# A decoder layer on one core: sum T2 in halves, another order of high parts, and two low parts on GpSimd, in the first up unit

## The chip, the cores and the metric

The kernel runs on one core of one Trainium2 chip. The time is what the device takes for one execution, in microseconds (us); lower is better. The core's engines run their own instruction streams side by side and meet at semaphores: TensorE (PE, with its weight loads PEld), VectorE (DVE), ScalarE (ACT), GpSimd (POOL) and SyncE (SP), which here only issues transfers.

## The reference, cut to what matters

One layer of a hybrid decoder on x of 1024 tokens by 1024 features, all float32. The change lies in the first half of the MLP (the up projection):

```
h = rms_norm(x) * (1.0 + scale2) + shift2
x = x + gate2 * (jnp.square(jax.nn.relu(h @ w_mlp_in[l])) @ w_mlp_out[l])   # w_mlp_in 1024 x 4096
return rms_norm(x) * final_norm_g
```

Ahead of it stand the conditioned norm, the combined projection, windowed attention, gated linear attention and the output projection, which the change does not touch.

## The kernel before, in words

**Precision.** A float32 operand is split in two: a high part (the value rounded to fp32r, one ScalarE copy) and a low part (value minus high part, one VectorE tensor_tensor). A product is three matmuls: high by high, high by low, low by high.

**Tiles.** The up projection h @ w_mlp_in is computed by a seven-product scheme of the Strassen-Winograd kind. h (turned, features on the partitions) is four quarters called 11, 12, 21 and 22, each 128 x 4 x 512: the first digit is the half of the features, the second the half of the tokens. Four sums are made of them: T1 = 12 - 11, T2 = 22 - T1, T3 = 22 - 12, T4 = 21 - T2. The sums lie in place of operands: T1 over 11, T3 over 12, T4 over T2 (`h_full`). The seven operands 11, 21, T1, T2, T3, T4, 22 each get a high and a low part, in two halves of 128x1024 (`form_hi`, L2182 on ScalarE, counted by s_hhi; `form_lo`, L1639 on VectorE, counted by s_hlo). The sums are `form_sum`, L1643, 128x2048, counted by s_hsum.

**Units.** There are NU = 8 units of weight columns. Each has seven weight forms (numbered f = 7u + i), of 128x1024 each: `wide_hi(f)`, L2146 on ScalarE, counted by s_whi, and `wide_lo(f)`, L1599 on VectorE, counted by s_wlo. Four buffers go round for them. TensorE runs the seven products in the order 11, 21, T1, T2, T3, T4, 22 (`up_product`, L1148), each in two halves m of 12 matmuls of 128x512, into two PSUM banks. Product i of unit u starts when s_wlo has reached f + 1 and, in unit 0 only, when the operand's low half has been counted by s_hlo: the first half before its k = 0, the second before its k = 2. The operands of h are made once, in unit 0, so this unit is the one in which TensorE waits for them.

**Banks.** Three products, T2's, T3's and T4's, add on top of one another in the same two banks as product 11 (X_UP). Between them ScalarE must copy what a bank holds: `kept`, L2214, 128x512 a bank. T2's product waits for the copy of 11's (s_p1), T3's for the copy of T2's (s_u2), T4's for the copy of T3's (s_u3).

**Order.** No scheduler decides anything: each engine's stream is in the order of its code. In unit 0, VectorE's goes: sum T1, low form 2, low T1, an affine (a scaled and shifted copy out of PSUM, 128x512, L1630), low form 3, sum T2, low T2, sum T3, low form 4, low T3, sum T4, low form 5, low T4. ScalarE's goes: high T1, three affines (L2166), the copies of 11's banks, high T2, high forms 4 and 5, high 22, high T3, the copies of T2's banks, high form 6, high T4. The tuple `H_HI_ORDER` repeats ScalarE's order, so that VectorE's `form_lo` waits for the right count of s_hhi. SP starts the loads of unit 1's weights when sums T2 and T4 are made, since they overwrite 11 and 21 (L531, L533). GpSimd has no work from the end of the linear attention to the down projection: it waits at s_prod, 14 * NU.

Of the kernel before, what the change touches and what calls it, by code (L numbers as in the profile page):

```python
# [87 lines left out]
UP_STARTS = (True, True, True, False, False, False, False)  # L88
UP_H = ("11", "21", "T1", "T2", "T3", "T4", "22")
H_ORDER = ("11", "21", "T1", "T2", "T3", "T4", "22")  # L90
H_HI_ORDER = ("11", "21", "T1", "T2", "22", "T3", "T4")
AFF_S = ((0, 0), (0, 2), (0, 4), (0, 5), (0, 6), (0, 7), (1, 0), (1, 2), (1, 4), (1, 5), (1, 6))
AFF_V = ((0, 1), (0, 3), (1, 1), (1, 3), (1, 7))
UP_P1, UP_P2, UP_P5, UP_P6, UP_P7, UP_P4, UP_P3 = range(NP)
# [62 lines left out]
def build(nc, x, c, w_ada, b_ada, w_in, w_gate_up, b_gate, gla_norm_g, attn_sinks, rel_bias,  # L157
# [236 lines left out]
    with block:  # L394

        @block.sync
        def _(sp):
# [130 lines left out]
                sp.wait_ge(s_free, G_O + 8 + t + 1)  # L528
                sp.dma_start(x1_rows[:, t, :], x1[:, t, :]).then_inc(s_x1_out[t // 4], 16)
            sp.wait_ge(s_hlo, 2 * (H_ORDER.index("T1") + 1))  # L530
            sp.wait_ge(s_hsum, 2)  # L531
            up_load(1, (0,))
            sp.wait_ge(s_hsum, 4)  # L533
            up_load(1, (1,))

            def hid_sums_store(u):
# [57 lines left out]
        @block.gpsimd  # L594
        def _(pool):
            pool.memset(ones[:, :], 1.0).then_inc(s_set, 1)
            pool.wait_ge(s_set, 1)
            pool.memset(rel_ext[BUCKETS:BUCKETS + 1, :], LOWEST).then_inc(s_set, 1)
            pool.wait_ge(s_set, 2)
            pool.memset(gate1[:, 512:D], 0.0).then_inc(s_set, 1)  # L600
            pool.wait_ge(s_ada_first[2 * NCK - 1], 32)
            pool.wait_ge(s_ada_full, 2)
            for part in range(2, 6):
                if part in gate_rows:
                    if part == 5:
                        pool.wait_ge(s_ada_sum, 1)
                    pool.dma_start(ada_b[0:1, :], b_ada[0:1, part * D:(part + 1) * D]).then_inc(s_ada_b, 16)
                for k in range(KT):
                    j = (part - 2) * KT + k
                    if j >= 4:  # L610
                        pool.wait_ge(s_ada_used, j - 3)
                    pool.dma_start(ada_w[:, j % 4, :], w_ada_d[:, k, part * D:(part + 1) * D])\
                        .then_inc(s_ada_w[j % 4], 16)
            pool.wait_ge(s_ada_used, 4 * KT)
            pool.memset(w_gate[:, :], 0.0).then_inc(s_set, 1)
            pool.wait_ge(s_set, 5)
            for r in range(COPIES):
                pool.dma_start(w_gate[r * COL:r * COL + RANK, :], w_gate_up[0]).then_inc(s_wg, 16)
            with nc.allow_non_contiguous_dma(reason="128 gains, one a partition"):
                pool.dma_start(gain_col, gla_norm_g[0].rearrange("(p a) -> p a", a=1)).then_inc(s_gn, 16)  # L620

            pool.wait_ge(s_gate_v, 10)
            pool.memset(a_mask[:, :, :], 0.0).then_inc(s_zeros, 1)
            pool.memset(state_a[:, :, :], 0.0).then_inc(s_zeros, 1)
            pool.memset(prob[:, :, 0:P], LOWEST).then_inc(s_zeros, 1)

            for n in range(NT):
                pool.wait_ge(s_g_copy, n + 1)
                pool.tensor_scalar(g_low[:, :], g_copy[:, :], -1.0, 0.0, ALU.mult, ALU.max).then_inc(s_pool, 1)
                pool.wait_ge(s_pool, n + 1)  # L630
                pool.wait_ge(s_sg_e, n + 1)
                pool.tensor_tensor(silu_g[:, :], silu_g[:, :], g_low[:, :], ALU.add).then_inc(s_sg_sum, 1)
                pool.wait_ge(s_sigmoid, n + 1)
                pool.tensor_tensor(silu_g[:, :], g_copy[:, :], silu_g[:, :], ALU.mult).then_inc(s_sg, 1)

            def dn_load(dst, block_of, q, landed):
                j, l = block_of
                for k in range(2):
                    pool.dma_start(dst[:, 2 * k:2 * k + 2, :],  # L639
                                   w_down_d[j, q][:, 2 * k:2 * k + 2, l * HALF:(l + 1) * HALF]).then_inc(landed, 16)  # L640

            def dn_ring_load(r):

                q = r % NQ
                if r >= 2:
                    step = (NQ * DN_P2, NQ * DN_P4, NQ * DN_P3)[(r - 2) // NQ] + (r - 2) % NQ
                    pool.wait_ge(s_dlo, 4 * step + 4)
                dn_load(dn_ring[r % 2], ((1, 0), (1, 0), (1, 1))[r // NQ], q, s_dn_ring[r % 2])

            def dn_ab_load(q):  # L650
                dn_load(dn_a[:, q], (0, 1), q, s_dn_ab[q])
                dn_load(dn_b[:, q], (1, 1), q, s_dn_ab[q])

            def residual_again(*tiles):
                for t in tiles:
                    pool.dma_start(x1[:, t, :], x1_rows[:, t, :]).then_inc(s_x1_back[t // 4], 16)

            pool.wait_ge(s_prod, 14 * NU)
            dn_ring_load(0)
            dn_ring_load(1)  # L660
            for form in range(NP):
                pool.wait_ge(s_hid_out[form], 16 * NU)
            for q in range(NQ):
                pool.wait_ge(s_dlo, 4 * q + 8)
                dn_ab_load(q)
            for r in range(2, 6):
                dn_ring_load(r)
            pool.wait_ge(s_dlo, 4 * (NQ * DN_P5 + 4))
            residual_again(0, 1, 2, 3)
            pool.wait_ge(s_dlo, 4 * (NQ * DN_P7 + 2))  # L670
            residual_again(4, 5, 6, 7)
            pool.dma_start(gain[:, :], final_norm_g.rearrange("(a d) -> a d", a=1).broadcast_to([P, D]))\
                .then_inc(s_gfin, 16)
            for r in range(6, 3 * NQ):
                dn_ring_load(r)
# [538 lines left out]
        def _(v):  # L1214
# [381 lines left out]
            def wide_lo(f):  # L1596

                v.wait_ge(s_whi, f + 1)
                v.tensor_tensor(up_lo[f % 4][:, :, :], up_form(f), up_hi[f % 4][:, :, :], ALU.subtract).then_inc(s_wlo, 1)  # L1599
# [85 lines left out]
            form_lo("T1")  # L1685
            v.wait_ge(s_x1_out[1], 64)
            affine(1, 7)
            wide_lo(3)
            v.wait_ge(*h_ready(1, 6))
            v.wait_ge(*h_ready(1, 7))  # L1690
            v.wait_ge(s_hsum, 1)
            form_sum("T2", "22", "T1")
            form_lo("T2")
            form_sum("T3", "22", "12")

# [42 lines left out]
            for u in range(NU):  # L1738
                f = NP * u
                if u > 0:  # L1740
                    up_add(u - 1, HID_S3, Z_UP, s_u2, UP_P3, s_c12)
                    wide_lo(f + 3)
                    hidden_sums(u - 1)
                    wide_lo(f + 4)
                    up_add(u, HID_11, Y_UP, s_p1, UP_P2, s_c11)
                    wide_lo(f + 5)
                    wide_lo(f + 6)
                else:
                    wide_lo(4)
                    form_lo("T3")  # L1750
                    v.wait_ge(s_hsum, 2)
                    form_sum("T4", "21", "T2")
                    wide_lo(5)
                    form_lo("T4")
                    up_add(u, HID_22, Z_UP, s_u3, UP_P5, s_c22)
                    wide_lo(6)
                    form_lo("22")
                    wide_lo(7)
                    up_add(u, HID_11, Y_UP, s_p1, UP_P2, s_c11)
                    v.wait_ge(s_hlo, 2 * NP)  # L1760
                next_sum(u + 1, 0)
                next_sum(u + 1, 1)
                if u > 0:
                    next_lo(f + 7)
                next_sum(u + 1, 2)
                if u == NU - 1:
                    down_lo(0)
                if u > 0:
                    up_add(u, HID_22, Z_UP, s_u3, UP_P5, s_c22)
                next_lo(f + 8)  # L1770
                next_sum(u + 1, 3)
                next_lo(f + 9)
# [146 lines left out]
        def _(a):  # L1919
# [250 lines left out]
            def form_hi(name):  # L2170

                for j in range(2):
                    ks = slice(2 * j, 2 * j + 2)
                    if name in ("11", "21", "22"):
                        half, k = int(name[1]) - 1, 4 * (int(name[0]) - 1) + 2 * j
                        a.wait_ge(*h_ready(half, k))
                        a.wait_ge(*h_ready(half, k + 1))
                    else:
                        a.wait_ge(s_hsum, int(name[1]))
                    if name == "T4":  # L2180
                        a.wait_ge(s_hlo, 2 * (H_ORDER.index("T3") + 1))
                    a.activation(h_hi[name][:, ks, :], h_full[name][:, ks, :], ACT.Copy).then_inc(s_hhi, 1)  # L2182
# [90 lines left out]
            for u in range(NU):  # L2273
                f = NP * u
# [8 lines left out]
                if u == 0:  # L2283
                    form_hi("T2")
                    wide_hi(4)
                    wide_hi(5)
                    form_hi("22")
                    form_hi("T3")
                    for m in range(2):
                        kept(HID_S3, u, m, UP_P6, s_u2)  # L2290
                    wide_hi(6)
# [99 lines left out]
```

## Time and profile before

| what | value |
|---|---|
| median of 3 runs | 1056.14 us (1054.41 to 1058.13) |
| the profiled execution's own time | 1054.87 us |
| its span, first to last instruction | 1053.1 us |
| TensorE busy | 1027.5 us, 98% |
| VectorE busy | 707.8 us, 67% |
| ScalarE busy | 474.5 us, 45% |
| GpSimd busy | 95.4 us, 9% |
| mean granted TensorE clock | 0.998 |

The trace's clock starts at the first instruction; the profiled execution is 1.8 us longer than its span. In rows of a timeline the first number is the start, the second the length from the first start to the last end of a run of like instructions, and x is their count; consecutive instructions on one engine overlap by about 0.1 us as shown, so a step is the difference of two starts. What stands in brackets is the engine's idle time before, and what ended it. TensorE's ends are modelled. Spans on GpSimd are rough. The granted clock is 1.00 of full speed through the up units.

### The profile page before, as it was taken

The numbers are of one execution on the slowest core, as the hardware profiler recorded it, in microseconds if no ns is written. First come the engines' busy times: TensorE is split into PE (matmuls) and PEld (weight loads), VectorE is DVE, ScalarE is ACT, GpSimd is POOL, SyncE is SP. The second block draws the span as 40 slices with busy tenths as digits, with TensorE's granted clock in tenths as the row PEclk, the third lists the DMA queues.
The fourth block names the chain that finished last, engine by engine and source line by source line (L and its number), as shares of the span: only waits on it lengthen the run. The fifth ranks groups of instructions, "written<-read, shape, count | busy, mean of one in ns | idle before, by whom it ended". The sixth has DMA issues, their size and how long they took to land.

```text
span 1053.1 us, 12994 instructions
## 1 busy us (share of the span) xinstructions
PE 1027.5 (98%) x5027; PEld 822.7 (78%) x5027; DVE 707.8 (67%) x926; ACT 474.5 (45%) x786; POOL 95.4 (9%) x123
## 2 busy tenths in 40 slices
PE   6999999999998999999999999999999999999997
PEld 4677887766676788878888888888888888888885
DVE  4576668788987264897555555554549963578886
ACT  7321012377776102765544544445453434335343
POOL 0111210022323000000000000000231000001100
PEclk9999999999999999999999999999999999999999
DMA  9977731300001613128345335327997332554633
GB/s 333 313 218 267 259 123 41 81 1 1 1 1 68 213 41 140 60 82 301 138 140 179 140 121 180 139 82 280 355 375 253 113 120 80 182 198 161 212 108 160
DMA packets 94052, 164.76 MB, mean 156 GB/s; under 512 B 15507, under 2 KB 44588, under 8 KB 93868
## 3 DMA queue, kind: packets, MB, share of 16 engines
q1 hardware_dynamic: 82108, 121.42, 33.9%
q0 software_dynamic: 11888, 42.55, 11.3%
q8 instruction: 40, 0.66, 0.3%
q14 instruction: 16, 0.13, 0.0%
HBM read 126.19 MB, written 39.33 MB: 157 GB/s over the span
## 4 chain that ended last, share of the span: by engine, by line
PE 55%; ACT 1%; DMA 1%; DVE 1%; issue 0%; SPq 0%; ACTq 0%
PE bank L1167 29%; PE bank L1148 26%; DMA dn_t<-in_w_mlp_out 1%; ACT h_hi_T L2182 0%; DVE h_T L1643 0%; ACT up_hi L2146 0%; ACT h_hi L2182 0%; DVE x L1845 0%; DVE up_lo L1599 0%; ACT hid_hi L2251 0%; ACT dn_hi L2254 0%; ACT hid L2214 0%; ACT out L2330 0%; DVE h L1630 0%; DVE x L1859 0%
## 5 line engine op out<-in xcount | busy, mean ns | idle before, releaser
L1167 PE MATMUL bank<-dn_hi,hid_hi 128*128 128x512 f32 x448 | 174.3, 389 | 0.0
L1167 PE MATMUL bank<-dn_lo,hid_hi 128*128 128x512 f32 x448 | 174.3, 389 | 0.0
L1167 PE MATMUL bank<-dn_hi,hid_lo 128*128 128x512 f32 x448 | 174.3, 389 | 0.0
L2251 ACT ACTIVATE hid_hi<-hid_raw 128x1024 fp32r<-128x1024 f32 x56 | 58.9, 1051 | 153.7 <-PE bank L1167 153.7
L1732 DVE TENSOR_TENSOR hid_lo<-hid_raw,hid_hi 128x1024 fp32r<-128x1024 f32 x56 | 68.3, 1220 | 84.7 <-ACT hid_hi L2251 84.7
L901 PE MATMUL bank<-w_hi,act_hi 128*128 128x512 f32 x256 | 103.1, 403 | 2.6 <-DVE w_lo L1233 2.5
L1148 PE MATMUL bank<-h_hi_T,up_hi 128*128 128x512 f32 x256 | 99.9, 390 | 1.8 <-DVE h_lo_T L1639 1.3
L1599 DVE TENSOR_TENSOR up_lo<-up_raw,up_hi 128x1024 fp32r<-128x1024 f32 x48 | 58.7, 1223 | 61.5 <-ACT up_hi L2146 61.5
L901 PE MATMUL bank<-w_hi,act_lo 128*128 128x512 f32 x256 | 99.9, 390 | 0.0
L901 PE MATMUL bank<-w_lo,act_hi 128*128 128x512 f32 x256 | 99.8, 390 | 0.0
L1148 PE MATMUL bank<-h_hi_T,up_lo 128*128 128x512 f32 x256 | 99.6, 389 | 0.0
L1148 PE MATMUL bank<-h_lo_T,up_hi 128*128 128x512 f32 x256 | 99.6, 389 | 0.0
L1167 PEld LDWEIGHTS bank<-dn_hi,hid_lo 128*128 128x128 f32 x448 | 84.1, 188 | 17.6
L1167 PEld LDWEIGHTS bank<-dn_lo,hid_hi 128*128 128x128 f32 x448 | 84.1, 188 | 17.5
L1167 PEld LDWEIGHTS bank<-dn_hi,hid_hi 128*128 128x128 f32 x448 | 84.1, 188 | 17.3
L2146 ACT ACTIVATE up_hi<-up_raw 128x1024 fp32r<-128x1024 f32 x48 | 50.5, 1056 | 73.3 <-PE bank L1148 55.4
L1935 ACT ACTIVATE w_hi<-raw 128x2048 fp32r<-128x2048 f32 x11 | 21.1, 1914 | 128.2 <-PE bank L698 83.7
L1148 PE MATMUL bank<-h_hi,up_hi 128*128 128x512 f32 x192 | 75.0, 390 | 0.3 <-DVE h_lo L1639 0.3
L1148 PE MATMUL bank<-h_hi,up_lo 128*128 128x512 f32 x192 | 74.7, 389 | 0.0
L1148 PE MATMUL bank<-h_lo,up_hi 128*128 128x512 f32 x192 | 74.7, 389 | 0.0
L901 PEld LDWEIGHTS bank<-w_hi,act_hi 128*128 128x128 f32 x256 | 48.0, 188 | 20.0 <-issue 6.7
L639 POOL DMA_DIRECT2D dn_ring<-in_w_mlp_out x24 | 17.5, 729 | 502.5 <-PE bank L1148 403.3
(252 smaller groups left out, 1933.8 us busy)
## 6 DMA issues: line engine op xcount, KB each, us to landing
hidden_forms<-hid SPq DMA_DIRECT2D x56, 512.0 KB, 3.1
hid_raw<-hidden_forms SPq DMA_DIRECT2D x56, 512.0 KB, 3.9
ada_w<-in_w_ada POOLq DMA_DIRECT2D x32, 512.0 KB, 6.8
up_raw<-in_w_mlp_in SPq DMA_DIRECT2D x32, 512.0 KB, 5.4
dn_ring<-in_w_mlp_out POOLq DMA_DIRECT2D x24, 512.0 KB, 6.0
raw<-in_w_in SPq DMA_DIRECT2D x34, 256.0 KB, 4.5
ada_chunk<-in_w_ada SPq DMA_DIRECT2D x16, 512.0 KB, 8.8
dn_t<-in_w_mlp_out POOLq DMA_DIRECT2D x16, 512.0 KB, 7.9
```

The costliest lines, as they stand in the source:

```text
L639: pool.dma_start(dst[:, 2 * k:2 * k + 2, :], w_down_d[j, q][:, 2 * k:2 * k + 2, l * HALF:(l + 1) * HALF]).then_inc(landed, 16)
L901: mm = pe.matmul(b, tok_act(i, 4 * part + k, t), wsl(j, s % 2)[:, k * HALF:(k + 1) * HALF], start=(part == 0 and n == 0), stop=(part == 1 ...
L1148: mm = pe.matmul(b, (up_hi, up_lo)[x][f % 4][:, k, m * P:(m + 1) * P], (h_hi, h_lo)[y][name][:, k, :], start=(UP_STARTS[i] and n == 0), st ...
L1167: mm = pe.matmul(b, (hid_hi, hid_lo)[x][n % 2][:, k, t * P:(t + 1) * P], (dn_hi, dn_lo)[y][n % 2][:, k, :], start=(first and i == 0), stop ...
L1599: v.tensor_tensor(up_lo[f % 4][:, :, :], up_form(f), up_hi[f % 4][:, :, :], ALU.subtract).then_inc(s_wlo, 1)
L1732: v.tensor_tensor(hid_lo[n % 2][:, ks, :], hid_raw[n % 2][:, ks, :], hid_hi[n % 2][:, ks, :], ALU.subtract).then_inc(s_dlo, 1)
L1935: a.activation(w_hi[:, par, :], raw[:, par, :], ACT.Copy).then_inc(s_hi, 1)
L2146: a.activation(up_hi[f % 4][:, :, :], up_form(f), ACT.Copy).then_inc(s_whi, 1)
L2251: a.activation(hid_hi[n % 2][:, ks, :], hid_raw[n % 2][:, ks, :], ACT.Copy).then_inc(s_dhi, 1)
```

## The change

In the first up unit alone:

- Sum T2 is made in two instructions of 128x1024 rather than one of 128x2048. ScalarE's high part of T2 starts on the first half when that is counted. The counts of s_hsum that others wait for move up by one; they are kept in a new table SUMS_BY.
- ScalarE makes the high part of T3 ahead of that of 22.
- The low parts of weight forms 3 and 4 are made by GpSimd (line 662 of the new file) with the same tensor_tensor instruction, 128x1024. It waits for the form's high part and for the count of the low part before. VectorE waits for both ahead of the low part of form 5.

```diff
-H_HI_ORDER = ("11", "21", "T1", "T2", "22", "T3", "T4")
+H_HI_ORDER = ("11", "21", "T1", "T2", "T3", "22", "T4")
+SUMS_BY = {"T1": 1, "T2": 3, "T3": 4, "T4": 5}
...
             sp.wait_ge(s_hlo, 2 * (H_ORDER.index("T1") + 1))
-            sp.wait_ge(s_hsum, 2)
+            sp.wait_ge(s_hsum, SUMS_BY["T2"])
             up_load(1, (0,))
-            sp.wait_ge(s_hsum, 4)
+            sp.wait_ge(s_hsum, SUMS_BY["T4"])
             up_load(1, (1,))
...
+            for f in (3, 4):
+                pool.wait_ge(s_whi, f + 1)
+                pool.wait_ge(s_wlo, f)
+                pool.tensor_tensor(up_lo[f % 4][:, :, :], up_form(f), up_hi[f % 4][:, :, :], ALU.subtract).then_inc(s_wlo, 1)
...
             affine(1, 7)
-            wide_lo(3)
             v.wait_ge(*h_ready(1, 6))
-            v.wait_ge(*h_ready(1, 7))
-            v.wait_ge(s_hsum, 1)
-            form_sum("T2", "22", "T1")
+            v.wait_ge(s_hsum, SUMS_BY["T1"])
+            for j in range(2):
+                if j == 1:
+                    v.wait_ge(*h_ready(1, 7))
+                ks = slice(2 * j, 2 * j + 2)
+                v.tensor_tensor(h_full["T2"][:, ks, :], h_full["22"][:, ks, :], h_full["T1"][:, ks, :], ALU.subtract)\
+                    .then_inc(s_hsum, 1)
             form_lo("T2")
             form_sum("T3", "22", "12")
...
                 else:
-                    wide_lo(4)
                     form_lo("T3")
-                    v.wait_ge(s_hsum, 2)
+                    v.wait_ge(s_hsum, SUMS_BY["T2"])
                     form_sum("T4", "21", "T2")
+                    v.wait_ge(s_wlo, 5)
                     wide_lo(5)
                     form_lo("T4")
...
-                        a.wait_ge(s_hsum, int(name[1]))
+                        a.wait_ge(s_hsum, SUMS_BY[name] - (1 if name == "T2" and j == 0 else 0))
...
                     wide_hi(5)
+                    form_hi("T3")
                     form_hi("22")
-                    form_hi("T3")
```

VectorE's order before, from sum T1 to the low part of T4. In the names h_70 is T1 (over 11), h_71 is 21, h_72 is 12 and then T3, h_73 is 22, h_T_74 is T2 and then T4; up_lo_100, 97 and 98 are the low parts of forms 3, 4 and 5.

```order
L1643 TENSOR_TENSOR h_70<-h_72,h_70 128x2048
L1599 TENSOR_TENSOR up_lo_99<-up_s_0_91,up_hi_95 128x1024
L1639 TENSOR_TENSOR h_lo_T_84<-h_70,h_hi_T_77 128x1024 x2
L1630 TENSOR_SCALAR h_73<-bank,small 128x512
L1599 TENSOR_TENSOR up_lo_100<-up_raw_89,up_hi_96 128x1024
L1643 TENSOR_TENSOR h_T_74<-h_73,h_70 128x2048
L1639 TENSOR_TENSOR h_lo_T_87<-h_T_74,h_hi_T_80 128x1024 x2
L1643 TENSOR_TENSOR h_72<-h_73,h_72 128x2048
L1599 TENSOR_TENSOR up_lo_97<-up_raw_89,up_hi_93 128x1024
L1639 TENSOR_TENSOR h_lo_T_85<-h_72,h_hi_T_78 128x1024 x2
L1643 TENSOR_TENSOR h_T_74<-h_71,h_T_74 128x2048
L1599 TENSOR_TENSOR up_lo_98<-up_raw_89,up_hi_94 128x1024
```

VectorE's order now, at the same place (the lines of the file have moved):

```order
L1649 TENSOR_TENSOR h_70<-h_72,h_70 128x2048
L1605 TENSOR_TENSOR up_lo_99<-up_s_0_91,up_hi_95 128x1024
L1645 TENSOR_TENSOR h_lo_T_84<-h_70,h_hi_T_77 128x1024 x2
L1636 TENSOR_SCALAR h_73<-bank,small 128x512
L1700 TENSOR_TENSOR h_T_74<-h_73,h_70 128x1024 x2
L1645 TENSOR_TENSOR h_lo_T_87<-h_T_74,h_hi_T_80 128x1024 x2
L1649 TENSOR_TENSOR h_72<-h_73,h_72 128x2048
L1645 TENSOR_TENSOR h_lo_T_85<-h_72,h_hi_T_78 128x1024 x2
L1649 TENSOR_TENSOR h_T_74<-h_71,h_T_74 128x2048
L1605 TENSOR_TENSOR up_lo_98<-up_raw_89,up_hi_94 128x1024
```

The low parts up_lo_100 and up_lo_97 are gone from VectorE, and sum T2 is two instructions. Nothing stands any more between sum T3 and the low part of T3.

ScalarE's order before, from T2's high part to T4's. Here h_hi_T_80 is T2's high part, h_hi_79 is 22's, h_hi_T_78 T3's, h_hi_T_81 T4's; hid_102 is the copy of the banks of T2's product; up_hi_93 and 94 belong to forms 4 and 5.

```order
L2182 ACTIVATE h_hi_T_80<-h_T_74 128x1024 x2
L2146 ACTIVATE up_hi_93<-up_raw_89 128x1024
L2146 ACTIVATE up_hi_94<-up_raw_89 128x1024
L2182 ACTIVATE h_hi_79<-h_73 128x1024 x2
L2182 ACTIVATE h_hi_T_78<-h_72 128x1024 x2
L2214 ACTIVATE hid_102<-bank 128x512 x2
L2146 ACTIVATE up_hi_95<-up_raw_89 128x1024
L2182 ACTIVATE h_hi_T_81<-h_T_74 128x1024 x2
```

ScalarE's order now, at the same place:

```order
L2191 ACTIVATE h_hi_T_80<-h_T_74 128x1024 x2
L2155 ACTIVATE up_hi_93<-up_raw_89 128x1024
L2155 ACTIVATE up_hi_94<-up_raw_89 128x1024
L2191 ACTIVATE h_hi_T_78<-h_72 128x1024 x2
L2191 ACTIVATE h_hi_79<-h_73 128x1024 x2
L2223 ACTIVATE hid_102<-bank 128x512 x2
L2155 ACTIVATE up_hi_95<-up_raw_89 128x1024
L2191 ACTIVATE h_hi_T_81<-h_T_74 128x1024 x2
```

T3's high part has changed places with 22's; the copy hid_102 stands behind both, as before.

## Rows read from the trace of the kernel before

**Rows 1.** The page, section 1: busy us, share of the span, instructions.
```profile
PE 1027.5 (98%) x5027; PEld 822.7 (78%) x5027; DVE 707.8 (67%) x926; ACT 474.5 (45%) x786; POOL 95.4 (9%) x123
```

**Rows 2.** Timeline of TensorE: products T1 (end), T2, T3, T4, 22 (start).
```profile
449.70 0.39 PE L1148 MATMUL bank<-h_hi_T,up_lo 128*128 128x512 f32 x1
451.40 0.47 PE L1148 MATMUL bank<-h_hi_T,up_hi 128*128 128x512 f32 x1 [1.31 <-DVE h_lo_T L1639]
...
456.69 0.39 PE L1148 MATMUL bank<-h_hi_T,up_lo 128*128 128x512 f32 x1
457.21 0.47 PE L1148 MATMUL bank<-h_hi_T,up_hi 128*128 128x512 f32 x1
...
462.91 0.47 PE L1148 MATMUL bank<-h_hi_T,up_hi 128*128 128x512 f32 x1
...
468.45 0.39 PE L1148 MATMUL bank<-h_hi,up_hi 128*128 128x512 f32 x1
```

**Rows 3.** Chain of waits: start, us, what; just ahead of T3's product.
```profile
456.64 0.49 ACT hid L2214
```

**Rows 4.** Timeline of VectorE, low T1 to low T3.
```profile
442.48 2.36 DVE L1639 TENSOR_TENSOR h_lo_T<-h,h_hi_T 128x1024 fp32r<-128x1024 f32 x2
444.76 0.81 DVE L1630 TENSOR_SCALAR h<-bank,small 128x512 f32<-128x512 f32 x1
445.48 1.21 DVE L1599 TENSOR_TENSOR up_lo<-up_raw,up_hi 128x1024 fp32r<-128x1024 f32 x1
446.62 2.28 DVE L1643 TENSOR_TENSOR h_T<-h,h 128x2048 f32<-128x2048 f32 x1
450.02 1.23 DVE L1639 TENSOR_TENSOR h_lo_T<-h_T,h_hi_T 128x1024 fp32r<-128x1024 f32 x1 [1.13 <-ACT h_hi_T L2182]
...
452.30 2.28 DVE L1643 TENSOR_TENSOR h<-h,h 128x2048 f32<-128x2048 f32 x1
454.50 1.22 DVE L1599 TENSOR_TENSOR up_lo<-up_raw,up_hi 128x1024 fp32r<-128x1024 f32 x1
455.72 1.23 DVE L1639 TENSOR_TENSOR h_lo_T<-h,h_hi_T 128x1024 fp32r<-128x1024 f32 x1
```

**Rows 5.** Timeline of ScalarE, the copies of 11's banks to those of T2's.
```profile
445.29 1.09 ACT L2214 ACTIVATE hid<-bank 128x512 f32<-128x512 f32 x2
448.93 2.00 ACT L2182 ACTIVATE h_hi_T<-h_T 128x1024 fp32r<-128x1024 f32 x2 [2.55 <-DVE h_T L1643]
450.84 1.99 ACT L2146 ACTIVATE up_hi<-up_raw 128x1024 fp32r<-128x1024 f32 x2
452.74 2.00 ACT L2182 ACTIVATE h_hi<-h 128x1024 fp32r<-128x1024 f32 x2
454.64 2.00 ACT L2182 ACTIVATE h_hi_T<-h 128x1024 fp32r<-128x1024 f32 x2
456.54 1.18 ACT L2214 ACTIVATE hid<-bank 128x512 f32<-128x512 f32 x2
```

**Rows 6.** GpSimd's groups by line: busy us, mean ns, idle before.
```profile
L625 POOL MEMSET prob<- 128x1024 f32 x1 | 1.0, 963 | 0.0
L600 POOL MEMSET gate<- 128x512 f32 x1 | 0.5, 530 | 0.1
```

**Rows 7.** Instructions of two lines: ns min/median/max, first and last start.
```profile
L632 POOL TENSOR_TENSOR silu_g<-silu_g,g_low x8: 1267/1268/2626, 219.1 to 333.8; 128x512 f32<-128x512 f32 x8
...
L1524 DVE TENSOR_SCALAR small<-small x8: 161/170/1251, 221.8 to 335.2; 128x4 f32<-128x4 f32 x8
```

**Rows 8.** Timelines of GpSimd and VectorE at 331 to 337 us.
```profile
331.67 2.00 POOL L629 TENSOR_SCALAR g_low<-g_copy 128x512 f32<-128x512 f32 x1 [9.17 <-ACT g_copy L2080]
333.75 2.63 POOL L632 TENSOR_TENSOR silu_g<-silu_g,g_low 128x512 f32<-128x512 f32 x1
...
332.95 2.28 DVE L1233 TENSOR_TENSOR w_lo<-raw,w_hi 128x2048 fp32r<-128x2048 f32 x1
335.15 1.25 DVE L1524 TENSOR_SCALAR small<-small 128x4 f32<-128x4 f32 x1
```

## The prediction

> **What bounds the kernel now.** I read the page first: TensorE has a matmul in flight for 1027.5 us, 98% of the span [rows 1]. So only a gap of TensorE, or a new one, can move the time. The second view is TensorE's timeline through the first up unit, where every edit lies. A product's first half is found by the 0.47 us matmul that follows a restart; three restarts stand there [rows 2]. T2's product starts at 451.40 after 1.31 us of idle behind a low part of T2. T3's starts at 457.21, 0.13 us after the last matmul's modelled end (456.69 + 0.39). T4's starts at 462.91. T4's product then runs 5.54 us to the start of 22's (468.45), which needs no restart. T3's takes 5.70, so 0.16 is lost at T4's start; T2's takes 5.81, so 0.27 is lost at T3's. A product without a restart takes 5.46, less by 0.47 - 0.39. All that can be won here is about 1.4 + 0.3 + 0.2 = 1.9 us, 0.2% of the time. I call the start of 22's product the gauge: what it is late, the end is late, as TensorE runs on from it nearly without a gap.
>
> Who starts T2's and T3's products? For T2 the chain is on two engines: sum T2 on VectorE ends at 446.62 + 2.28 = 448.90, ScalarE makes the high part from 448.93, VectorE starts the first low half at 450.02, it ends at 451.25, and TensorE starts 0.15 later [rows 2, 4, 5]. For T3 the timeline's own releaser is not printed, so I took the chain of waits: ahead of 457.21 stands ScalarE's copy of T2's finished bank, L2214 [rows 3]. That copy is queued on ScalarE behind 22's and T3's high parts [rows 5]. The low half of T3 (455.72 + 1.23 = 456.95, rows 4) was ready 0.1 us before the copy. So T3's product has two gates, and the copy is the later one.
>
> **The change, part by part.**
> Removed from VectorE ahead of sum T2: the low part of form 3, one step of 446.62 - 445.48 = 1.14 us; and behind sum T3 that of form 4, 1.22 us [rows 4]. Sum T2 in two halves: the first half ends 1.22 us after it begins, and ScalarE can start then, so T2's first low half follows the sum's start after 1.22 + 0.04 + 1.06 + 0.04 + 1.23 = 3.6 us rather than 4.6 (446.62 to 451.25). The split itself costs one instruction's start, 2 x 1.14 against 2.20 for steps back to back: 0.08.
>
> Moved on ScalarE: T3's high part (two steps of 0.95) ahead of 22's (two more). Before, T3's high part began when 22's had ended; the copy came 1.90 after T3's began (456.54 - 454.64). Now the copy comes four steps, 3.80 us, after T3's begins, and T3's begins only when sum T3 ends. This is a new cost of the order itself: sum T3's end to T3's product becomes 0.04 + 3.80 + 0.58 + 0.09 = 4.51 us, where it was 457.21 - 454.58 = 2.63.
>
> If nothing else happened: sum T2 starts at 445.48, low half one ends near 449.1, so T2's product is bound by TensorE itself at 449.93 (the end of T1's product: 449.70 + 0.23), 1.47 early. Sum T3 then starts near 450.12 and ends at 452.41; T3's product starts at 452.41 + 4.51 = 456.92, only 0.29 early. Two products of 5.54 and 5.46 (one restart) bring the gauge to 467.92, 0.53 early. The swap gives back most of what the split wins.
>
> Added on GpSimd: two tensor_tensor of 128x1024. The trace has none of that size. The nearest rows are 128x512 with two SBUF inputs: 1.268 is their median [rows 7]. A start cost of 0.1 follows from the memsets (0.963 for 1024, 0.530 for 512: 0.433 per 512) [rows 6]. Bounds: not below 1.27, since it has twice the elements, and 2.54 at twice the 512 one. I take 2 x 1.27 - 0.1 = 2.44, nearest to the upper row. GPSIMD Engine Reference of the Trainium skill, section 3.1, gives 4497 ns for 2048 elements; by half of it an estimate would be 2.25, between the bounds.
>
> Does it run beside VectorE? One place shows it [rows 8]. GpSimd's L632 begins at 333.75 while VectorE's L1233, 128x2048 with two SBUF inputs, runs (332.95 to 335.23). L632 then takes 2.63 instead of 1.27 and ends 1.15 after L1233 does. VectorE's next instruction, L1524, has 0.17 as its median [rows 7] and takes 1.25 there, ending at 336.40 just behind GpSimd's 336.38. So the two shut each other out for whole instructions, and GpSimd, once it waits, goes ahead of VectorE's next. That VectorE's own tensor_tensor is held by a running GpSimd one is the mirror of the first half of this, which no row shows.
>
> The Trainium skill, SBUF — State Buffer, section "Who interferes with whom", says that a VectorE instruction with two SBUF inputs contends with a GpSimd instruction that reads SBUF, and that the one issued first has the shared ports for its whole length. By that rule the offload is no relief, since 1.22 us on VectorE turn into a longer exclusion; the 2.63 of L632 agrees.
>
> I therefore charge each GpSimd instruction 2.44 - 0.12 = 2.32 of exclusion (0.12 is what 1.27 exceeds the 1.15 by). The blocked 128x1024 then ends 1.05 after it: 1.22 less the 0.17 that it has already spent starting.
>
> Form 3's low part waits for form 2's, done when VectorE moves on at 442.48. GpSimd waits from 442.6, gets the ports when T1's first low half ends (442.48 + 1.22 = 443.70), holds to 446.02. T1's second low half ends at 447.08 (was 444.84). TensorE, which starts T1's product at 449.93 - 5.46 = 444.47 and needs that half a quarter of the way on, waits some 1.4 us there; that replaces the wait ahead of T2. Affine 0.72 later sum T2 starts, 447.72; its halves end at 448.94 and 450.08. T2's first low half ends at 451.31, T2's product starts at 451.46, 0.06 late: the split is used up.
>
> ScalarE: T2's high halves from 448.98 and 450.12, then form 4's high part, ending at 452.12. GpSimd starts 0.08 later (it starts that much behind its releaser, 333.67 to 333.75), at 452.20. VectorE is in T2's second low half until 452.44 with sum T3 behind it. GpSimd is in time by 0.24, holds 452.44 to 454.76. Sum T3 ends 2.28 - 0.17 = 2.11 later, near 456.88 (was 454.58). T3's product starts at 456.88 + 4.51 = 461.39, 4.18 late. T4's path follows: low T3 ends by 460.3, sum T4 by 462.5, T4's first low half by 465.0, all ahead of T3's product's end at 466.93. So T4's and 22's restart with no wait, and the gauge is at 461.39 + 5.54 + 5.46 = 472.39 against 468.45: **+3.9 us**.
>
> SP's loads of the next unit wait for sums T2 and T4, which end at 450.1 and 462.5 (448.9 and 460.3 before). They move less than TensorE does, so nothing is late behind them. Sum: the profiled execution 1054.87 + 3.9 = 1058.8; on the median, 1056.14 + 3.9 = **1060.0 us**.
>
> **Rivals.**
> (a) One exclusion counts, not both. If GpSimd comes 0.24 us later, sum T3 goes first and ends at 454.64. GpSimd works while ScalarE makes T3's high part, and the copy gates: T3's product at 459.15, the gauge +1.7. If VectorE's queued instruction always goes first, GpSimd takes its turn at the affine (one PSUM input) and again behind sum T3: sum T2's first half ends at 448.2, sum T3 at 453.9, the gauge +0.9. For it: the 0.24 is small against 10 us of reckoned steps. Against: in rows 8 the waiting GpSimd went first. Time 1057.0 to 1057.8.
> (b) Not slower: GpSimd and VectorE run side by side. Place: the same two instructions; price 0 each; gauge -0.5, 1055.6. It decides when T1's second low half still ends near 444.9. For it: L629, a one-input GpSimd instruction (331.67 to 333.67), overlapped 0.7 us of L1233, which still took 2.28. Against: L632 and L1524. All waits gone would be -1.9 (1054.2), but the copy behind 22's high part forbids it.
> (c) The edge is larger: GpSimd's instruction is longer than 2.54. Each 0.1 on it is 0.2 on the gauge, since T3's chain holds both; at 3.0 it is +5.0, 1061.1. The rows speak against it, though none writes fp32r from GpSimd.
>
> **How the numbers follow.** Forecast 0.48, (a) 0.27, (b) 0.18, (c) 0.07. The forecast's bounds: with GpSimd at 2.2 to 2.54 it is +3.5 to +4.1, so 1059.5 to 1060.3; at the low end of 1.27, two times 1.17 less, near +1.6, as in (a). 0.3% is 3.2 us, about what a measurement of this kernel tells from no change; the three runs before spread from 1054.41 to 1058.13, so +3.9 falls beyond it some 7 times in 10. Slower 0.34 + 0.06 + 0.02 = 0.42. Faster has only (b) with luck and a share of noise: 0.06. Within 0.3%: 0.52. The range takes in (b) at 1055.6 and (c) at 1061.1, with a little of the runs' spread: 1054.8 to 1062.0; the forecast's own is 1058.5 to 1061.5.
>
> **What would show it.** GpSimd's L662 with spans of about 3.5 us from 442.6 and 2.6 us from 452.2; a T1 low half (L1645) and sum T3 (L1649) each drawn out by about 2.3; TensorE waiting near 1.4 us inside T1's product and over 4 us ahead of T3's, released there by ScalarE's copy (now L2223). Wrong would be: both L662 near 2.4 with VectorE's durations unchanged (then b); L662 drawn out behind sum T3 (then a); T3's product released by its own low part rather than the copy.

## The result and the profile after

| | median us | lowest to highest | runs |
|---|---|---|---|
| before, in the same measurement | 1055.97 | 1054.41 to 1058.13 | 5 |
| changed | 1062.13 | 1060.70 to 1062.68 | 5 |
| changed, a second measurement | 1062.58 | 1059.72 to 1063.53 | 5 |
| before, in the second one | 1055.85 | 1054.30 to 1057.93 | 21 |

The changed kernel is slower: ratio 1.0058, 95% interval 1.0047 to 1.0068, or +6.2 us; in the second measurement 1.0061 (1.0046 to 1.0075). Forecast were +3.9 and 1060.0, with a range that ended at 1062.0. The direction was right, the size was not.

The page of the changed kernel: TensorE's share has gone from 98% to 97%, and its span from 1053.1 to 1060.4 us. That answers to [rows 1].

```profile
span 1060.4 us, 12998 instructions
...
PE 1030.1 (97%) x5027; PEld 824.3 (78%) x5027; DVE 710.1 (67%) x925; ACT 474.7 (45%) x786; POOL 101.3 (10%) x125
```

TensorE's waits in the changed kernel (line waiting, releaser, us in total, times, longest). The second row is the wait inside T1's product, the first the one ahead of T3's.

```profile
PE bank L1154 <- ACT hid L2223: 4.2, 1, 4.2
PE bank L1154 <- DVE h_lo_T L1645: 1.1, 1, 1.1
```

TensorE's timeline of the changed kernel, answering to [rows 2]:

```profile
449.50 0.50 PE L1154 MATMUL bank<-h_hi_T,up_hi 128*128 128x512 f32 x1 [1.08 <-DVE h_lo_T L1645]
...
453.81 0.47 PE L1154 MATMUL bank<-h_hi_T,up_hi 128*128 128x512 f32 x1
...
463.71 0.76 PE L1154 MATMUL bank<-h_hi_T,up_hi 128*128 128x512 f32 x1 [4.18 <-ACT hid L2223]
464.28 0.63 PE L1154 MATMUL bank<-h_lo_T,up_hi 128*128 128x512 f32 x1
...
476.23 0.39 PE L1154 MATMUL bank<-h_hi,up_hi 128*128 128x512 f32 x1
```

Look at the second column: behind the 4.18 us wait a matmul of 128x512 takes 0.63 us, not 0.39. The first number has to be read against the first matmul of the up units, since the traces arrive there at different times (429.95 before, 432.34 here). From it, T2's product starts after 21.47 us (21.45 before), T3's after 31.37 (27.26), and 22's, the gauge, after 43.89 (38.50).

VectorE and GpSimd, answering to [rows 4, 8]:

```profile
444.88 4.57 DVE L1645 TENSOR_TENSOR h_lo_T<-h,h_hi_T 128x1024 fp32r<-128x1024 f32 x2
...
450.10 2.34 DVE L1700 TENSOR_TENSOR h_T<-h,h 128x1024 f32<-128x1024 f32 x2
452.43 2.36 DVE L1645 TENSOR_TENSOR h_lo_T<-h_T,h_hi_T 128x1024 fp32r<-128x1024 f32 x2
454.71 4.49 DVE L1649 TENSOR_TENSOR h<-h,h 128x2048 f32<-128x2048 f32 x1
```

```profile
445.03 3.34 POOL L662 TENSOR_TENSOR up_lo<-up_raw,up_hi 128x1024 fp32r<-128x1024 f32 x1 [105.86 <-DVE up_lo L1605]
454.56 2.50 POOL L662 TENSOR_TENSOR up_lo<-up_raw,up_hi 128x1024 fp32r<-128x1024 f32 x1 [6.19 <-ACT up_hi L2155]
```

The pair of low halves of T1 takes 4.57 us where it took 2.36, sum T3 4.49 where it took 2.28: 2.21 us each, exactly where a GpSimd instruction stands. GpSimd came at 454.56, when T2's second low half had 0.23 us left, and went ahead of sum T3, which was next.

ScalarE, answering to [rows 5]: T3's high part, 22's, the copy. The copy starts 3.80 us after T3's high part.

```profile
459.24 2.00 ACT L2191 ACTIVATE h_hi_T<-h 128x1024 fp32r<-128x1024 f32 x2 [3.81 <-DVE h L1649]
461.15 1.99 ACT L2191 ACTIVATE h_hi<-h 128x1024 fp32r<-128x1024 f32 x2
463.04 1.06 ACT L2223 ACTIVATE hid<-bank 128x512 f32<-128x512 f32 x2
```

The granted clock by stretches. The changed kernel's first trace, then that of its second measurement. The columns are the stretch, its length, TensorE's busy time and count of matmuls, the granted clock, the DMA share and GB/s.

```profile
459.00:463.00 4.00, 0.53 (x3) 1.00 0.00 0
463.00:465.00 2.00, 1.28 (x3) 0.65 0.00 0
465.00:467.00 2.00, 2.00 (x6) 0.50 0.40 105
467.00:471.00 4.00, 4.00 (x19) 1.00 0.60 209
```

```profile
459.00:463.00 4.00, 0.35 (x1) 0.87 0.00 0
463.00:467.00 4.00, 4.00 (x10) 0.50 0.52 160
467.00:471.00 4.00, 4.00 (x15) 0.77 0.29 102
471.00:475.00 4.00, 4.00 (x20) 1.00 0.02 4
```

0.50 is the lower of the clock's two levels, 1.2 GHz. In both traces the clock falls while TensorE still waits, some 0.1 us before the end of the long wait in the first and 0.7 us before it in the second, and is back at 1.00 about 3.4 and 6.9 us later. So in the second trace the fall lasts about twice as long: T3's and T4's products together take 13.92 us there (462.64 to 476.56), 12.52 in the first trace, and 11.24 before.

So the span of the first trace, 7.3 us longer, divides as follows. 0.8 us stand ahead of 336 us, in the start-up, and are not the change's, as the second trace has -0.3 there. 1.6 are a fall of the clock at 336 us, which the changed trace has and that of before has not (experiments y2 and y3). Up to T3's product it is 4.1, over T3's and T4's products 1.3, and behind them -0.5 (0.33 of it is a wait that before had at 730 us and that is missing here).

### The profile page after: what moved, and what is told of

Read it like the earlier page. It is cut to its first block, busy times and chain, and to the rows that moved or that the text cites. A ratio compares the mean times of both kernels' runs of the same rounds, so it can differ in the third digit from the quotient of the medians.

```text
span 1060.4 us, 12998 instructions
## 1 busy us (share of the span) xinstructions
PE 1030.1 (97%) x5027; PEld 824.3 (78%) x5027; DVE 710.1 (67%) x925; ACT 474.7 (45%) x786; POOL 101.3 (10%) x125
## 4 chain that ended last, share of the span: by engine, by line
PE 87%; DVE 7%; issue 2%; SPq 2%; ACT 1%; DMA 1%; DVEq 0%; ACTq 0%
PE bank L1173 29%; PE bank L1154 27%; PE bank L907 16%; PE bank L704 8%; DVE prob L1502 2%; PE bank L823 2%; PE bank L949 1%; DMA ada_chunk<-in_w_ada 1%; SPq L406 1%; PE bank L971 1%; DVE h_lo_T L1645 1%; DVE h L1649 1%; DVE prob L1485 1%; PE bank L777 0%; DVE state_b L1521 0%
## 5 line engine op out<-in xcount | busy, mean ns | idle before, releaser
L1605 DVE TENSOR_TENSOR up_lo<-up_raw,up_hi 128x1024 fp32r<-128x1024 f32 x46 | 56.3, 1224 | 61.9 <-ACT up_hi L2155 61.9
L1154 PEld LDWEIGHTS bank<-h_hi_T,up_hi 128*128 128x128 f32 x256 | 48.4, 189 | 16.7 <-issue 5.1
```

Source lines behind the costliest of these rows:

```text
L1154: mm = pe.matmul(b, (up_hi, up_lo)[x][f % 4][:, k, m * P:(m + 1) * P], (h_hi, h_lo)[y][name][:, k, :], start=(UP_STARTS[i] and n == 0), st ...
```

## The experiments

Theory A is the prediction's: each GpSimd instruction shuts VectorE out for 2.2 to 2.3 us, and the copy behind 22's high part adds 1.9 more to T3's product. To it comes now: behind the long wait T3's product runs in part at half clock. The rivals are named in each expectation. "Gauge" in the table is the time from the first up matmul to the start of 22's product, read from one trace of each.

| kernel | T3's product | gauge | against before | median / before, us | ratio (95%) |
|---|---|---|---|---|---|
| before | 27.26 | 38.50 | | | |
| changed | 31.37 | 43.89 | +5.4 | 1062.13 / 1055.97 | 1.0058 (1.0047 to 1.0068) |
| changed again | 31.37 | 45.29 | +6.8 | 1062.58 / 1055.85 | 1.0061 (1.0046 to 1.0075) |
| x1_old_order | 29.50 | 42.11 | +3.6 | 1059.75 / 1056.05 | 1.0036 (1.0023 to 1.0049) |
| x2_no_gpsimd | 28.09 | 39.07 | +0.6 | 1056.93 / 1056.05 | 1.0011 (1.0002 to 1.0020) |
| x3_split_only | 26.39 | 37.62 | -0.9 | 1055.29 / 1056.05 | 0.9993 (0.9984 to 1.0001) |
| x4_gpsimd_only | 30.75 | 43.21 | +4.7 | 1060.68 / 1056.05 | 1.0044 (1.0031 to 1.0057) |
| x5_order_only | 29.15 | 40.16 | +1.7 | 1057.68 / 1055.43 | 1.0020 (1.0011 to 1.0029) |
| x6_warm | 31.38 | 42.38 | +3.9 | 1059.59 / 1055.43 | 1.0040 (1.0028 to 1.0053) |
| z1_later_gpsimd | 29.16 | 40.16 | +1.7 | 1058.03 / 1056.11 | 1.0021 (1.0010 to 1.0031) |
| z2_memsets | 26.39 | 37.61 | -0.9 | 1054.57 / 1056.11 | 0.9990 (0.9981 to 0.9999) |

### x1: the old order on ScalarE

```diff
-H_HI_ORDER = ("11", "21", "T1", "T2", "T3", "22", "T4")
+H_HI_ORDER = ("11", "21", "T1", "T2", "22", "T3", "T4")
...
-                    form_hi("T3")
                     form_hi("22")
+                    form_hi("T3")
```

> The changed kernel with ScalarE's old order (the high part of 22 ahead of T3's); sum T2 in halves and the two low parts on GpSimd stay. Theory A (exclusion on both GpSimd instructions, plus the copy queued behind 22's high part): sum T3 still ends 2.3 us late, but the copy then comes 1.9 and not 3.8 us after T3's high part starts, so T3's product starts near 2.3 us late instead of 4.2, with a wait of TensorE of about 2.4 us. Whether the granted clock falls behind a wait of 2.4 us is open: +2.0 us against before if it does not, +3.5 if it does. Rival B (the order of the high parts is free, the low part of T3 is the gate and GpSimd alone costs all): as the changed kernel, +6 us.

T3's product comes 2.24 us late rather than 4.11, and the medians are 3.7 us apart. Its trace, ScalarE: the copy starts 1.91 after T3's high part.

```profile
458.50 2.00 ACT L2191 ACTIVATE h_hi_T<-h 128x1024 fp32r<-128x1024 f32 x2 [1.93 <-DVE h L1649]
460.41 1.06 ACT L2223 ACTIVATE hid<-bank 128x512 f32<-128x512 f32 x2
```

Theory A holds, with the clock's fall behind a 2.31 us wait in this trace (T3's product takes 7.17 us, T4's 5.44). Rival B, that the order is free, is out.

### x2: the low parts back on VectorE; x3: the split alone

x2 takes the loop out of GpSimd, and `v.wait_ge(s_wlo, 5)` with it, and puts `wide_lo(3)` and `wide_lo(4)` back where they were. x3 does this and takes the old order of x1 too.

```diff
-            for f in (3, 4):
-                pool.wait_ge(s_whi, f + 1)
-                pool.wait_ge(s_wlo, f)
-                pool.tensor_tensor(up_lo[f % 4][:, :, :], up_form(f), up_hi[f % 4][:, :, :], ALU.subtract).then_inc(s_wlo, 1)
...
             affine(1, 7)
+            wide_lo(3)
...
                 else:
+                    wide_lo(4)
                     form_lo("T3")
```

> The changed kernel with the low parts of forms 3 and 4 back on VectorE at their old places; sum T2 in halves and T3's high part ahead of 22's stay. Theory A: no exclusion, sum T2's halves start at the old 446.6, T2's product starts 1.0 us earlier, sum T3 ends 1.1 us earlier, the copy comes 3.8 us after it and T3's product starts 0.8 us late: +0.6 us against before, no fall of the clock. Rival B: no cost without GpSimd, -1.0 us. A third rival (the loss comes from somewhere else, for instance ahead of the up units): still +5 to +6 us.

> Only sum T2 in halves, all else as before. Theory A: T2's product 1.0 us earlier, bound by VectorE (sum halves, then the low half); T3's product gated by the copy and the low part, 0.9 us earlier; 22's product 1.0 us earlier: -1.0 us against before. Rival (the product of T3 gives it back, since ScalarE's queue has no slack): 0.

x2: T3's product 0.83 late, x3: 0.87 early; both were forecast (0.8 and 0.9). In x3 two of TensorE's waits in the first up unit are 0.3 us ahead of T3's product and 0.2 ahead of T2's, where before had 0.3 and 1.3:

```profile
PE bank L1149 <- ACT hid L2219: 0.3, 1, 0.3
...
PE bank L1149 <- DVE h_lo_T L1640: 0.2, 1, 0.2
```

The measured -0.8 us of x3 has an interval that just takes in no change; the trace's -0.9 and z2, below, agree with a gain. The loss of the changed kernel is not in the split, and outside the up unit x2 shows none. One of x2's twelve runs took 1060.22 us, 3 us above the next, at a mean clock of 0.995, so the clock seems to have fallen there once more, though no fall was expected.

### x4: GpSimd alone; x5: the order alone

x4 is the kernel before with the same loop on GpSimd and without `wide_lo(3)` and `wide_lo(4)` on VectorE. x5 is the kernel before with the two lines of the order exchanged.

> Only the low parts of forms 3 and 4 on GpSimd, all else as before. Theory A: T1's second low half drawn out by 2.3 us, sum T2 whole starts 1.1 us late, T2's product 1.1 us late; the second GpSimd instruction goes ahead of sum T3, which ends 3.4 us late; T3's product starts 3.3 us late with a wait of 2.6 us: +3.1 us against before, +4.6 if the granted clock falls behind that wait. Rival B (side by side): -0.3 us or less, as T3's product is gated by ScalarE.

> Only T3's high part ahead of 22's on ScalarE, all else as before. Theory A: sum T3 ends at 454.6 as before, four steps of 0.95 us stand between it and the copy of T2's banks, T3's product starts 1.9 us late after a wait of 2.2 us: +1.65 us against before, and 1.5 more if the granted clock falls behind it. Rival B (the low part of T3 is the gate): 0 or a little below.

Measured +4.6 and +2.3 us (medians). x4's two waits, on the copy and, in two places, on low parts:

```profile
PE bank L1153 <- ACT hid L2218: 2.3, 1, 2.3
PE bank L1153 <- DVE h_lo_T L1644: 2.3, 2, 1.2
```

x4's T3 product is 3.49 us late (forecast 3.3), and the clock fell behind that wait in its trace. x5's is 1.89 late (forecast 1.9). In x5's trace the clock stayed at 1.00 behind a wait of 1.98 us, and the trace's gauge is +1.7; the median lies 0.6 above that. Rival B is out in both.

### x6: TensorE kept busy in the wait

```diff
+            def keep_warm(count):
+                for n in range(count):
+                    pe.matmul(bank[5][:, :], up_hi[3][:, n % 4, 0:P], h_hi["T2"][:, n % 4, :], start=(n == 0),
+                              stop=(n == count - 1), skip_group_check=True)
...
+                        if u == 0 and (i, m) == (UP_P7, 0):
+                            keep_warm(16)
                         up_product(u, i, m)
```

> The changed kernel with 16 matmuls of 128x512 (3.6 us at full clock) on the operands of T2's product, into a bank that nothing uses here, put between T2's and T3's products, where TensorE waits 4.2 us. Their result is read by nobody. Theory A says that 1.5 us of the loss are matmuls of T3's product at half clock behind the wait: with TensorE busy there the granted clock stays at 1.00, T3's product starts at the same time and the whole is 1.5 us faster than the changed kernel, about +4.4 us against before. Rival (the granted clock falls whatever TensorE does there, or the extra loss lies elsewhere): as the changed kernel, +5.9.

Its trace: the 16 extra matmuls fill the wait but 0.61 us, and T3's product starts when it did (31.38 us behind the first up matmul). The stretches show the clock.

```profile
458.25 3.79 PE L1162 MATMUL bank<-h_hi_T,up_hi 128*128 128x512 f32 x16
462.64 0.47 PE L1154 MATMUL bank<-h_hi_T,up_hi 128*128 128x512 f32 x1 [0.61 <-issue]
```

```profile
462.00:464.00 2.00, 1.39 (x7) 1.00 0.00 0
464.00:468.00 4.00, 4.00 (x20) 1.00 0.78 251
```

The gauge is 42.38, 3.88 us behind before: the prediction's +3.9, to the tenth. Without the fall of the clock the forecast's sum comes out. The time is +4.2 us (medians) and not +6.2 to +6.7. Against 43.89 and 45.29 in the two traces of the changed kernel, the fall of the clock cost 1.5 us in one and 2.9 in the other.

### y1, y2, y3: the changed kernel again, and the wait at 333 us

y1 is the changed kernel as it stands, measured a second time. y2 is the kernel before with nine extra matmuls (the trace shows two records for each) where TensorE waits 2.3 us for a low part of the output weights; y3 has the same and the split of T2.

```diff
-            pe.wait_ge(s_lo, SLOT_O + 1)
             pe.wait_ge(s_sc_free, 4 * NT)
+            for n in range(9):
+                pe.matmul(bank[0][:, 0:P], ident[:, :], tri[:, :], start=(n == 0), stop=(n == 8))
+            pe.wait_ge(s_lo, SLOT_O + 1)
             out_pass(0, 0, 0)
```

> The changed kernel once more, beside the others of this call. The phases of its first trace give +4.1 us up to T3's product, +1.3 for T3's and T4's products (half clock), -0.5 behind them: +4.9 to +5.2 us against before, at the same number of falls of the clock behind the attention. The first measurement was +6.2. If 1 us of that was the chip or the day, this comes out near +5; if the changed kernel has one more cost outside the up units, near +6 again.

> The kernel before with nine float32 matmuls of 128x128 (about 0.22 us each, 2.0 us) into a bank that is overwritten next, where TensorE waits 2.3 us for a low part of the output weights at 333 us. Nobody reads their result. Theory: in some executions the granted clock falls to half for 3.4 us behind this wait and costs 1.6 us, which is why the times of every kernel here lie in two groups. With TensorE busy the fall goes: all executions in the faster group, 1054.5 to 1054.9, the median 0.6 to 1.5 us below before. Rival (falls come at random times, not from this wait): the groups stay, and the median is that of before.

> Sum T2 in halves alone, with low parts on VectorE and the old order of high parts, and the same nine matmuls at 333 us. If both theories hold the gains add: 0.9 us and 0.6 to 1.5 us, so 1053.6 to 1054.0 in all executions, 1.5 to 2.4 us below before's median. Rival: only the 0.9 of the split.

y1 came out at +6.7 us: above the +5 of its first branch and above the "near +6" of its second, and the second branch's reason, a cost outside the up units, does not hold. Its trace is 0.3 us earlier than before's at 316 us, and takes the same time to 0.1 us from the gauge to the end (584.7 us in both); the clock's fall behind the long wait was just longer. One of its five runs had 1059.72, with a mean clock of 0.997; the others had 0.993 to 0.995 and 1062.55 to 1063.53.

y2: 1055.17 against 1055.85, ratio 0.9994 (0.9985 to 1.0003), so the median alone shows nothing. The spread does: its 11 runs lie in 1054.68 to 1055.55, at clocks of 0.998 to 0.999, while the 21 runs of before measured beside it lie in two groups, 9 in 1054.30 to 1054.98 (0.998 to 0.999) and 12 in 1055.75 to 1057.93 (0.996 to 0.997). With the wait filled the slower group is gone, though its times came out up to 0.7 us above what I expected. Its trace:

```profile
333.76 2.17 PE L1073 MATMUL bank<-tri,ident 128*128 128x128 f32 x18
336.26 0.50 PE L901 MATMUL bank<-w_hi,act_hi 128*128 128x512 f32 x1 [0.33 <-DVE w_lo L1235]
```

y3: 1054.14 us (1053.67 to 1054.46, 11 runs), ratio 0.9986 (0.9977 to 0.9995), -1.7 us. Seven of its eleven runs lie above the 1054.0 that was to be the top, by up to 0.5 us. It has the lowest median and the lowest ratio of the study, and is faster than both kernels of the case; against z2, below (0.9990, 0.9981 to 0.9999), the intervals overlap, and nothing is shown.

### z1: GpSimd later; z2: GpSimd only writes

z1 is the changed kernel with one wait more.

```diff
                 pool.wait_ge(s_wlo, f)
+                if f == 4:
+                    pool.wait_ge(s_hsum, SUMS_BY["T3"])
```

> The changed kernel with one more wait: GpSimd starts the low part of form 4 only when sum T3 is made, so it works while VectorE waits for T3's high part. The same instructions on all engines, only their meeting is moved. Theory A (the length of sum T3 is exclusion, and GpSimd goes first when it comes first): sum T3 (L1649) has its 2.28 us again, T3's product starts 29.2 us after the first up matmul and not 31.4 (27.3 before), with a wait of 2.0 us; +1.8 us against before, plus 1.5 in those executions in which the clock falls behind that wait. Rival (GpSimd's part is late in any case, or is slow by itself): +4 or more.

Its trace, VectorE and then GpSimd: sum T3 has its 2.28 us back, and GpSimd takes 2.41 us with VectorE idle at its start; the first low half of T3 is drawn out instead (3.67 for the pair).

```profile
453.57 2.28 DVE L1651 TENSOR_TENSOR h<-h,h 128x2048 f32<-128x2048 f32 x1
456.98 3.67 DVE L1647 TENSOR_TENSOR h_lo_T<-h,h_hi_T 128x1024 fp32r<-128x1024 f32 x2 [1.13 <-ACT h_hi_T L2193]
```

```profile
456.02 2.41 POOL L664 TENSOR_TENSOR up_lo<-up_raw,up_hi 128x1024 fp32r<-128x1024 f32 x1 [8.80 <-DVE h L1651]
```

T3's product 29.16 (forecast 29.2), +1.9 us by the medians. The same instructions cost +1.9 us rather than +6.2 or +6.7 by meeting elsewhere: by the traces 2.2 us of the difference are sum T3's, and the rest, 1.5 us in the first and 2.9 in the second, is the clock.

z2 is x3 with this on GpSimd. Not shown below are two waits that keep the borrowed buffer in order: one on GpSimd ahead of the loop, one on ScalarE before that buffer is used.

```diff
+            for f in (3, 4):
+                pool.wait_ge(s_whi, f + 1)
+                if f == 3:
+                    pool.wait_ge(s_wlo, f)
+                for m in range(2):
+                    pool.memset(hid_sb[HID_12][:, :, :], 0.0).then_inc(s_zeros, 1)
+                    pool.wait_ge(s_zeros, 3 + 2 * (f - 3) + m + 1)
```

> Sum T2 in halves alone (low parts on VectorE, old order), and GpSimd runs two memsets of 128x1024 at each of the two moments at which the changed kernel starts its tensor_tensor there, 1.9 us of GpSimd writing, reading nothing, into a buffer that is overwritten later. If a GpSimd instruction that only writes leaves VectorE's two-input instructions alone, as the page SBUF - State Buffer of the Trainium skill has it, VectorE's durations stay and the time is that of the split alone, -0.8 us against before. If any GpSimd instruction excludes them, a low half of T1 and one of T2 or sum T3 are drawn out by 0.9 to 1.9 us each, and it is +2 to +3.5 us.

Its trace, GpSimd and then VectorE beside it:

```profile
444.20 1.97 POOL L665 MEMSET hid<- 128x1024 f32 x2 [105.88 <-DVE up_lo L1609]
452.69 1.97 POOL L665 MEMSET hid<- 128x1024 f32 x2 [6.52 <-ACT up_hi L2160]
```

```profile
444.05 2.36 DVE L1649 TENSOR_TENSOR h_lo_T<-h,h_hi_T 128x1024 fp32r<-128x1024 f32 x2
...
452.80 2.28 DVE L1653 TENSOR_TENSOR h<-h,h 128x2048 f32<-128x2048 f32 x1
```

Not one VectorE instruction is longer than in x3, and the gauge is that of x3 to 0.01 us. The median is 1.5 us below before's, where 0.8 was expected; the interval (0.9981 to 0.9999) takes in both.

So a GpSimd instruction that only writes does not shut VectorE's two-input instructions out, and the changed kernel's, which reads two inputs, does. The section "Who interferes with whom" of SBUF — State Buffer (the Trainium skill) draws the line between GpSimd instructions that read SBUF and those that only write it. z2 agrees with the second half. With the first half the changed kernel agrees and [rows 8] do not: GpSimd's L629 reads SBUF (one input) and ran for 0.7 us beside VectorE's two-input L1233, and neither was longer (2.00 and 2.28 us, where the medians of these lines are 2.00 and 2.29). All thirteen traces have this overlap. GpSimd's spans are rough, and no run put a one-input GpSimd instruction into the up unit, so it is open whether reading alone is enough.

The trace of before says more on who is held than the one place that the prediction read. GpSimd and then VectorE, in two places:

```profile
233.97 1.27 POOL L632 TENSOR_TENSOR silu_g<-silu_g,g_low 128x512 f32<-128x512 f32 x1
238.85 1.29 POOL L634 TENSOR_TENSOR silu_g<-g_copy,silu_g 128x512 f32<-128x512 f32 x1 [3.62 <-ACT silu_g L2087]
...
232.81 2.58 DVE L1496 TENSOR_SCALAR prob<-prob,small 128x256 f32<-128x256 f32 x4
238.96 1.28 DVE L1479 SCALAR_TENSOR_TENSOR prob<-bank,bias 128x512 f32<-128x512 f32 x2
```

In the first, VectorE's tensor_scalar on SBUF is drawn out beside a GpSimd tensor_tensor: four of L1496 take 2.58 us, where the four at 247.33 take 1.14, and the longest one is 1.44 where the median is 0.35. That happens at six of the eight L632. In the second, a VectorE instruction that reads one input from PSUM and one from SBUF runs beside GpSimd's two-input L634, and both keep their length (0.68 us each for L1479, 1.29 for L634, as their medians).

## Why the prediction was wrong

Taken by its own steps:

- **The exclusion: right.** Forecast about 2.3 us on a T1 low half and on sum T3; measured 2.21 on each. A VectorE tensor_tensor is held by a running GpSimd one, which no row of the prediction showed; the trace of before had VectorE's tensor_scalar drawn out beside one in six more places (L1496, above), and the prediction read one place only. GpSimd's spans were to be near 3.5 and 2.6 us and are 3.34 and 2.50; undisturbed at its start, one takes 2.41 (z1), where 2.44 was reckoned.
- **The race for the second one: right.** GpSimd was to be in time by 0.24 us; it was by 0.23. z1 shows what rival (a) would have been: the forecast's +1.7 in its gauge.
- **T2's product: right.** 0.06 us late forecast, 0.02 measured; the wait inside T1's product was to be 1.4 and is 1.1.
- **The copy as the gate: right.** 4.18 us late forecast for T3's product, 4.11 measured; with the old order 2.24 (x1), the order alone 1.89 (x5).
- **"So T4's and 22's restart with no wait, and the gauge is at 461.39 + 5.54 + 5.46": this step failed.** It gave T3's product its length at full clock, 5.54 us, right behind a wait that the same text put at 4.2 us. It took 7.08 us in the first trace and 8.47 in the second. The sum +3.9 lacked a term of 1.5 to 2.9 us: the matmuls behind the long wait at half clock. It was put at nothing without a reason; the prediction does not mention the clock. With the wait filled (x6) T3's product takes 5.56 us and the gauge is +3.88.
- **The bound:** the range ended at 1062.0, with the top set by a longer GpSimd instruction (rival c), not by the clock. The measured 1062.13 lies 0.1 outside. Had it fallen inside, that would have been luck, since rival (c) did not happen. Rival (b) is out.
- **"0.3% is what a measurement tells from no change":** the spread before, 1054.41 to 1058.13, was taken as noise. Much of such a spread is two groups about 1.6 us apart, with and without a fall of the clock behind the wait at 333 us (y2, y3).

Shown: the exclusion, that a memset does not make it, who goes first, the copy's part, and that TensorE's idleness at the long wait brings the fall, as it goes when the wait is filled. Not settled: what decides between a fall of 1.5 and one of 2.9 us, and from what length on a wait brings one. In the traces the clock fell behind the waits of 2.31 and 2.33 us ahead of T3's product in x1 and x4, and behind most of those of 2.34 us at 336 us. It stayed at 1.00 behind 1.98, 1.98 and 2.01 us in x2, x5 and z1. Some of their other runs look like a fall there too, by their times and mean clocks: one of x2's twelve (1060.22 us, 0.995), two of x5's twelve (1058.97 and 1059.33, 0.994 and 0.996), two of z1's eight (1059.31 and 1059.99, both 0.996). No trace was taken of them.

## What to carry to other kernels

A two-input tensor_tensor on SBUF that is handed to GpSimd does not run beside VectorE's two-input work but in its place, and 1.8 times as long (2.2 us of exclusion for 1.2): put it where VectorE reads one of its inputs from PSUM, idles, or has slack, and count who stands first when they meet. Where TensorE is the bound, price a new wait twice: its length, and the matmuls behind it at half clock (seen here behind waits of 2.3 us and more, 1.5 to 2.9 us of loss). Filling an unavoidable wait with matmuls into a free bank gave the second part back in all three kernels that did it (x6, y2, y3). When a step is moved ahead in an in-order queue, ask what the step it overtakes, and all behind it, had been releasing: here a 0.6 us copy.

## What the runs showed of the hardware that I had not expected

- A wait of 4.2 us of TensorE cost up to 2.9 us more behind it. The wait of 2.3 us that ends near 336 us costs 1.6 more in some executions (96.27 us in the changed kernel's trace against 94.66 in before's, from the restart there to the first up matmul), and makes a kernel's times fall into two groups; 12 of before's 21 runs beside y2 are in the slower one.
- Two GpSimd memsets of 128x1024 beside VectorE's tensor_tensor left every duration as it was (2.36, 2.28 us), where one GpSimd tensor_tensor there cost 2.21.
- A waiting GpSimd instruction went first even when it had come only 0.23 us before VectorE's next one could start.
- A one-input GpSimd instruction on SBUF (L629) left a two-input one of VectorE as it was, in 0.7 us of overlap.
